# Two mixers that run on into their expert layers: normalising by token tile, turned tokens scaled in their copy, experts chosen on logits

## The reference

```
h = layer_norm(ALPHA * h + mix(h), ln_mix_g[l], ln_mix_b[l])     # mix: Mamba-2 (l = 0), differential attention (l = 1)
h = layer_norm(ALPHA * h + hier_moe(h), ln_ffn_g[l], ln_ffn_b[l])

def hier_moe(x):                                  # 4 groups of 8 experts, d_ff = 512
    g_prob = softmax(x @ w_group);  g_sel = argmax(g_prob)
    e_logits = (x @ w_expert)[the 8 of group g_sel]
    top_p, top_i = top_k(softmax(e_logits), 2);  top_p /= sum(top_p)
    weight = g_prob[g_sel] * top_p
    return sum over the 2 experts of weight * (silu(x @ w_gate[e]) * (x @ w_up[e])) @ w_down[e]
```

## The kernel before, in words

| step | engine | line |
|---|---|---|
| slots: mask of token to slot | VectorE | L958 |
| pick: gather the 32 tokens of e, turned, as h_rows x mask (32 passes) | TensorE | L966 |
| xg: copy them out of PSUM | ScalarE | L974 |
| gate and up product | TensorE | L981 |
| silu; times up; turn; copy (hT) | ScalarE, VectorE, TensorE, VectorE | L990, L996, L1002, L1010 |
| down product, and copy of its rows | TensorE; both | L1020, L1030, L1039 |

## Time and profile before

### The profile page before, as it was taken

One profiled execution on the slowest core, in us unless ns is written; L12 is line 12 of the kernel. 1 busy time (PEld: TensorE's weight loads), 2 busy tenths in 40 slices (PEclk: granted clock), 3 DMA queues, 4 the chain that ended last, 5 costly groups with the idle time before them and its releaser, 6 DMA issues. The chain is left out here.

```text
span 2371.8 us, 32407 instructions
## 1 busy us (share of the span) xinstructions
PE 2086.6 (88%) x13361; PEld 1391.1 (59%) x13361; DVE 690.8 (29%) x2051; ACT 372.8 (16%) x989; POOL 98.5 (4%) x96
## 2 busy tenths in 40 slices
PE   8999969999888697689888888697899989879997
PEld 7686456656556344366665565344588544448863
DVE  4355231111111316321111111367222014722211
ACT  2122111101111014011111111114121001312100
POOL 0112010000000100100000000100001000000110
PEclk9999957877888797778788888798899989889998
DMA  9332357999999941359999999631243333213420
GB/s 339 131 118 107 119 204 316 424 426 426 426 426 425 372 146 67 107 212 424 426 427 426 426 427 422 257 142 36 93 168 143 122 141 142 72 71 142 142 89 27
DMA packets 111421, 566.58 MB, mean 239 GB/s; under 512 B 11304, under 2 KB 14558, under 8 KB 78558
## 3 DMA queue, kind: packets, MB, share of 16 engines
q1 hardware_dynamic: 111326, 565.26, 59.8%
HBM read 564.19 MB, written 1.05 MB: 238 GB/s over the span
## 5 line engine op out<-in xcount | busy, mean ns | idle before, releaser
L981 PE MATMUL ps<-ring,arena 128*32 128x256 f32 x3968 | 261.9, 422 | 59.4 <-issue 38.4
L2148 PE MATMUL ps<-arena,ring 128*128 128x256 f32 x1408 | 308.0, 382 | 1.6 <-DVE arena L245 1.6
L2148 PEld LDWEIGHTS ps<-arena,ring 128*128 128x128 f32 x1408 | 270.0, 192 | 39.7 <-DVE arena L245 2.4
L966 PEld LDWEIGHTS ps<-arena 128*128 128x128 f32 x2048 | 247.6, 201 | 28.5 <-issue 25.5
L966 PE MATMUL ps<-arena 128*128 128x32 f32 x2048 | 255.1, 285 | 2.8 <-DVE arena L958 2.8
L1445 PE MATMUL ps<-ring,arena 128*128 128x512 f32 (+1 forms) x576 | 250.7, 595 | 2.5 <-DVE arena L245 1.6
L981 PEld LDWEIGHTS ps<-ring,arena 128*32 128x32 f32 x3968 | 154.9, 122 | 166.6 <-issue 115.3
L267 PE MATMUL ps<-ring,arena 128*128 128x512 f32 x544 | 236.8, 597 | 1.6 <-DVE arena L1485 0.8
L1020 PE MATMUL ps<-ring,arena 128*32 128x256 f32 x1984 | 179.3, 522 | 26.8 <-issue 25.8
L1445 PEld LDWEIGHTS ps<-ring,arena 128*128 128x128 f32 x576 | 110.1, 193 | 136.0 <-issue 132.3
L267 PEld LDWEIGHTS ps<-ring,arena 128*128 128x128 f32 x544 | 103.9, 192 | 131.7 <-issue 129.1
(11 more groups left out here) (297 smaller groups left out, 1713.8 us busy)
## 6 DMA issues: line engine op xcount, KB each, us to landing
ring<-in_moe_w_gate_dram SPq DMA_DIRECT2D x62, 2048.0 KB, 19.0
ring<-in_moe_w_up_dram SPq DMA_DIRECT2D x62, 2048.0 KB, 23.5
ring<-in_moe_w_down_dram SPq DMA_DIRECT2D x62, 2048.0 KB, 19.9
ring<-in_w_up_dram SPq DMA_DIRECT2D x22, 2048.0 KB, 7.8
ring<-in_ssm_w_in_dram SPq DMA_DIRECT2D x12, 2048.0 KB, 10.0
ring<-in_w_in_dram SPq DMA_DIRECT2D x10, 2048.0 KB, 13.5
ring<-in_w_down_dram SPq DMA_DIRECT2D x10, 2048.0 KB, 7.7
ring<-in_attn_w_qkv_dram SPq DMA_DIRECT2D x6, 2048.0 KB, 20.4
```

The lines of the kernel that those rows point to most:

```text
L966: mm = nc.tensor.matmul(ps[:, 4, k * CAP:(k + 1) * CAP], h_rows[:, tt, k, :], slots[:, b, tt, :], start=(tt == 0), stop=(tt == TT - 1))
L981: mm = nc.tensor.matmul(ps[j * CAP:(j + 1) * CAP, 5, 0:256], xg[:, b, k * CAP:(k + 1) * CAP], w[:, k, (j % 2) * 256:(j % 2 + 1) * 256], st ...
L2148: mm = nc.tensor.matmul(ps[:, n % 4, 0:SEQ], w[:, k, k4 * P:(k4 + 1) * P], xT_mlp[:, k, :], start=(k == 0), stop=(k == KD - 1))
```

## The change

- Expert layers have no block of their own. The functions of `moe` become `make_experts`, and each engine runs on from the mixer's stream into them; only the block ends after expert layers 0 and 1 are left.
- The norm is made per token tile. Tile 0 is summed, normalised and turned while TensorE still has products of tile 1 to do; for that the last pieces of the mixer's product are reordered. ScalarE normalises one half of the features of a tile, VectorE the other, without g and b, into `normed`, whose features are reordered in that write.
- `normed` is turned, and g and b are put in as scale and bias where the turned tokens are copied out of PSUM (`act_affine_T`, `dve_affine_T`; g and b are loaded as vectors along the partitions). GpSimd writes h = normed * g + b later (`pool_affine`), beside the first experts.
- The gathering reads `normed`, so the gathered tokens get g and b afterwards: VectorE makes xg by two instructions, where ScalarE made one copy.
- Groups and experts are chosen on the logits. The weights come from two exponential sums, exp(e_i - e_max) / (sum_group * sum_expert), made while TensorE gathers expert 0.
- ALPHA * h into PSUM moves from expert 0 to expert 3. Expert 1's weights and the router's are loaded earlier, where their places come free.
- From expert layer 0 to attention the same per-half norm and scaled copies are used; the qkv weights are loaded in the reordered row order.

Its core (`...` marks what is left out):

```diff
+        def pe_turn_normed(pe, tt, use=0):
+            pe.wait_ge(half_act.sem, half_act.at(2 * use + tt + 1))
+            pe.wait_ge(half_dve.sem, half_dve.at(2 * use + tt + 1))
+            for j in range(2):
+                for k in range(4):
+                    mm = nc.tensor.transpose(ps[:, 4 + 2 * tt + j, k * P:(k + 1) * P], normed[:, tt, 4 * j + k, :], ident)
+                mm.then_inc(n_turned.sem, 1)
+        def act_affine_T(act, tt, xT, which, use=0):
+            act.wait_ge(n_turned.sem, n_turned.at(4 * use + 2 * tt + 1))
+            for k in range(4):
+                ins = nc.scalar.activation(xT[:, k, tt * P:(tt + 1) * P], ps[:, 4 + 2 * tt, k * P:(k + 1) * P],
+                                           ACT.Identity, bias=vec[:, which, 1, k:k + 1], scale=vec[:, which, 0, k:k + 1])
+            ins.then_inc(xT_act.sem, 1)
+        def pool_affine(pool):
+            for tt in range(TT):
+                hv = h[:, tt, :].rearrange("p (q k) -> p k q", k=KD)
+                g, b = (rows_gb[:, i, :].rearrange("p (q k) -> p k q", k=KD) for i in range(2))
+                Q(nc.gpsimd.tensor_tensor(hv, normed[:, tt, :, :], g, ALU.mult))
+                ins = nc.gpsimd.tensor_tensor(hv, hv, b, ALU.add)
...
+            def dve_tokens(self, dve):
+                self.dve_sums(dve, 0, 0)
+                self.dve_sums(dve, 0, 1)
+                self.dve_norm(dve, 0)
+                self.dve_sums(dve, 1, 0)
+                dve.wait_ge(vectors_loaded.sem, 8 * 16)
+                dve_affine_T(dve, 0, xT_route, self.which)
+                self.dve_sums(dve, 1, 1)
+                self.dve_norm(dve, 1)
+                V(nc.vector.memset(lg, NEG))
+                self.dve_group(dve, 0)
+                dve_affine_T(dve, 1, xT_route, self.which)
+                self.dve_experts(dve, 0)
+                self.dve_group(dve, 1)
+                self.dve_experts(dve, 1)
+                dve.wait_ge(chosen.sem, chosen.at(2))
+                self.dve_positions(dve)
...
+            def step_xg(dve, s, v, prev, b):
+                dve.wait_ge(s["picked"].sem, v(s["picked"]))
+                if prev:
+                    dve.wait_ge(s["gateup"].sem, prev(s["gateup"]))
+                x = xg[:, b, :].rearrange("p (k c) -> p k c", k=KD)
+                nc.vector.tensor_tensor(x, ps[:, 4, 0:KD * CAP].rearrange("p (k c) -> p k c", k=KD),
+                                        bcast(g_mix, CAP), ALU.mult).then_inc(s["xg_scaled"].sem, 1)
+                dve.wait_ge(s["xg_scaled"].sem, v(s["xg_scaled"]))
+                nc.vector.tensor_tensor(x, x, bcast(b_mix, CAP), ALU.add).then_inc(s["xg"].sem, 1)
...
+                step_pick(pe, m, lambda s: s.at(1), 0)
+                head.pe_tally(pe)
+                for i in range(4):
+                    expert(0, i)
...
+                step_slots(dve, m, lambda s: s.at(1), None, 0, 0)
+                head.dve_weights(dve)
+                nc.vector.tensor_scalar(alpha_id, ident, ALPHA, None, ALU.mult).then_inc(alpha_ready.sem, 1)
+                step_xg(dve, m, lambda s: s.at(1), None, 0)
...
+            def experts_pool(pool):
+                pool.wait_ge(crowd.sem, crowd.at(1))
+                pool.wait_ge(half_act.sem, half_act.at(2))
+                pool.wait_ge(rows_loaded.sem, rows_loaded.at(32))
+                pool_affine(pool)
...
-                 ("out", 2, 0), ("out", 2, 1), ("out", 2, 2), ("turn_y", 6), ("turn_y", 7), ("out", 2, 3),
-                 ("out", 3, 0), ("out", 3, 1), ("out", 3, 2), ("out", 3, 3)]
+                 ("out", 2, 0), ("out", 2, 1), ("out", 2, 2), ("turn_y", 6), ("turn_y", 7),
+                 ("out", 3, 0), ("out", 3, 1), ("out", 2, 3), ("out", 3, 2), ("turn_normed", 0), ("out", 3, 3)]
...
+                for i, part in ((0, 0), (0, 1), (1, 0), (1, 1), (0, 2), (0, 3), (1, 2)):
+                    out_piece(i, part)
+                pe_turn_normed(pe, 0)
+                out_piece(1, 3)
+                head.pe_route(pe, 0)
+                pe_turn_normed(pe, 1)
+                head.pe_route(pe, 1)
+                head.pe_counts(pe)
+                experts.pe(pe)
```

More of the change, by code:

```diff
@@ L195, in hybrid_stack @@
         c_moe = [add_experts(0)]
-        c_qkv = [add(cols8(qkv_w, 512 * i, 512 * i + 512)) for i in range(6)]
+        c_qkv = [add(rows8_cols(qkv_w, 512 * i, 512 * i + 512)) for i in range(6)]
         c_wo = [add(rows4(o_w, i)) for i in range(2)]
@@ new lines, in dve_row_norm, with act_half @@
+        def dve_row_norm(tts):
+            mv, v, r = ln_mv[:, tts, :], ln_v[:, tts], ln_r[:, tts]
+            for tt in range(tts.start, tts.stop):
+                V(nc.vector.bn_aggr(ln_mv[:, tt, :], ln_stats[:, tt, :, :]))
+            V(nc.vector.tensor_scalar(v, mv[:, :, 1], EPS, None, ALU.add))
+            rsqrt(r, v, ln_t[:, tts])
+            return nc.vector.scalar_tensor_tensor(ln_b[:, tts], mv[:, :, 0], -1.0, r, ALU.mult, ALU.mult)
+        def act_half(tt, src, n_view):
+            return nc.scalar.activation(n_view, src, ACT.Identity, bias=ln_b[:, tt:tt + 1], scale=ln_r[:, tt:tt + 1])
@@ new lines, in dve_half @@
+        def dve_half(tt, src, n_view):
+            return nc.vector.tensor_scalar(n_view, src, ln_r[:, tt:tt + 1], ln_b[:, tt:tt + 1], ALU.mult, ALU.add)
+        def pe_turn_normed(pe, tt, use=0):
[5 more added lines that the diff above has]
+                mm.then_inc(n_turned.sem, 1)
@@ new lines, in act_affine_T, with dve_affine_T @@
+        def act_affine_T(act, tt, xT, which, use=0):
[4 more added lines that the diff above has]
+            ins.then_inc(xT_act.sem, 1)
+        def dve_affine_T(dve, tt, xT, which, use=0):
+            dve.wait_ge(n_turned.sem, n_turned.at(4 * use + 2 * tt + 2))
+            for k in range(4, 8):
+                ins = nc.vector.tensor_scalar(xT[:, k, tt * P:(tt + 1) * P], ps[:, 5 + 2 * tt, (k - 4) * P:(k - 3) * P],
+                                              vec[:, which, 0, k:k + 1], vec[:, which, 1, k:k + 1], ALU.mult, ALU.add)
+            ins.then_inc(xT_dve.sem, 1)
@@ new lines, in hybrid_stack @@
+        xT_first = area(6144, KD, SEQ)
+        STEP_SEMS = ("slots", "picked", "xg_scaled", "xg", "gateup", "silu", "hidden", "turned", "hT", "down", "rows_act",
+                     "rows_dve", "back", "back_turned", "back_copied")
+        MAIN = {n: sem("moe_" + n) for n in STEP_SEMS}
+        OVER = [{n: sem(f"over{layer}_" + n) for n in ("loaded", "shifted", "combined") + STEP_SEMS} for layer in range(2)]
+        alpha_ready, token_combined = sem("alpha_ready"), sem("token_combined")
+        w1_loaded, tail_stats = sem("w1_loaded"), sem("tail_stats")
@@ L715, in _ @@
                         copy_group(*s)
-                act_norm(act)
+                head.act_norm(act)
+                experts.act(act)
             @block.gpsimd
@@ L896, in _ @@
                 dve.wait_ge(dt_act.sem, 5)
-                dve_add_sums(dve, len(c_wout), True, 0)
-                dve_layer_norm(dve, lnp)
+                head.dve_tokens(dve)
+                experts.dve(dve)
         turn_done()
-        sums_done(len(c_wout))
-        norm_done()
-        W4 = 4 * CAP
-        route_pe, route_act, route_dve = sem("route_pe"), sem("route_act"), sem("route_dve")
-        router_loaded = sem("router_loaded")
-        STEP_SEMS = ("slots", "picked", "xg", "gateup", "silu", "hidden", "turned", "hT", "down", "rows_act",
-                     "rows_dve", "back", "back_turned", "back_copied")
@@ L1426, in hybrid_stack @@
-        moe(0, t["ln_ffn_g"][0], t["ln_ffn_b"][0])
+        summed.advance(3)
+        experts.done()
         projected, projected_copied = sem("projected"), sem("projected_copied")
```

1116 lines of the change are left out of this document (589 added, 527 removed).

## The result

Four runs of each kernel beside one another give 2337.4 us (2337.0 to 2338.4) for the changed kernel and 2366.5 us (2364.6 to 2372.5) for the kernel before: a ratio of 0.9873 with a 95% interval of 0.9854 to 0.9892, 29.1 us less. The second time that both ran side by side it was 2334.6 (2332.7 to 2336.0) and 2366.8 us, ratio 0.9865 (0.9844 to 0.9887). I had forecast 2327 us, range 2306 to 2344, from a gain of 38 us. The sign and the range hold; the gain was 9 us smaller. The profiled executions stand at 2373.6 and 2337.9 us (span 2371.8 and 2336.1).

What follows compares the result with a forecast made beforehand. The prediction took the weight stream to pace both expert loops, with TensorE just behind. Gains of 15, 16.5 and 6.5 us, 38 in all, off the 2364.99 us median gave 2327 us, range 2306 to 2344.

Steps and rivals of the forecast that it cites:

- What counts is when a stream starts: Expert loops: the weight stream paces them, so earlier starts gain about 15 us in layer 0, 16.5 us in layer 1.
- T to the first gate and up product, 26.9 us: Mixer-to-expert hand-over, from the last mixer product's end: 26.9 us against 43.5, a gain of 16.6 us.
- GpSimd's price: Behind expert 0's gathering: VectorE's x+b waits for GpSimd's whole operation, 2.2 us; an estimated 3.3 us by the skill's rule.
- T later by 2.3 and 1.2 us: End of the last mixer product: moved transposes delay it 1.2 us, and in the Mamba mixer ScalarE's copies another 1.1 us.
- The alpha products and DMA running dry: Layer 0: moving them off expert 4's load path saves 6.2 us, but DMA runs dry for 4.3 us, then 1 us.
- In the loop: cost nothing: Every expert: x*g and x+b, 1.0 us, hide beside the 1.93 us down product, leaving 0.9 us.
- Expert layer 0 to attention, 6.5 us: Third hand-over, to the first qkv product: 10.7 us against 17.2, a gain of 6.5 us.
- The sum: Whole kernel: gains of 15, 16.5 and 6.5 us make 38 us, giving 2327 us.
- 1 (clock stays full): Hand-overs: TensorE's clock stays at its full level, 8 and 6 us more gain, 2313 us; chance 0.17.
- 2: Hand-overs: GpSimd holds VectorE back more than once, costing 4 us a layer; gain 24 us, 2341 us; chance 0.15.
- 3: Expert loops: the streams have slack and starts don't count; only 6.5 us is left, 2358.5 us; chance 0.04.
- 4: Every expert: x*g and x+b outlast the down product, gate and up waits; slower, 2383 us; chance 0.04.

Runs made afterwards that it cites:

- experiment 3: Changed kernel with expert 4's gate and up loads issued only after expert 2's down product, both layers; 9.5 us above experiment 4.
- experiment 4: Changed kernel with expert 3's gate and up loads issued only after expert 0's down product, both layers; 2336.6 us.
- Experiment 8: Changed kernel with exponentials and routing weights put back ahead of positions and slot masks; 4.5 us above experiment 6.
- experiment 1: Changed kernel with GpSimd's scale and bias of h held until VectorE has made expert 1's slot masks; 2329.0 us.
- experiment 11: Changed kernel with eight extra unread x*g instructions on VectorE in every expert; 11.6 us slower than experiment 10.
- experiment 9: Changed kernel with the alpha*h products moved from expert 3 to expert 1, ahead of expert 4's load; 2334.4 us.
- experiment 10: Changed kernel with four extra unread x*g instructions on VectorE in every expert; 2333.5 us.
- Experiment 2: Changed kernel with unread filler products (8, 3, 5, 1, 4) in TensorE's gaps at both mixer-to-expert hand-overs; time moved by 1.3 us.
- experiment 5: The kernel before, run again unchanged; 2366.8 us.
- experiment 6: The changed kernel, run again unchanged; 2334.6 us.
- experiment 12: Changed kernel with unread TensorE fillers (5, 2, 3, 1, 2) and GpSimd's second tile held behind expert 3's masks; 2325.5 us, 0.9831 of the kernel before.

## Why the prediction was right, and where its numbers were off

**What counts is when a stream starts: right, with the wrong mark named.** Experiments 3 and 4 show it. I had computed with expert 4's load as well as with the first gate and up product; only the first is the start.

**T to the first gate and up product, 26.9 us: the terms right, two sized too small.** Measured 28.67, four times within 0.02. By terms: to the router's start 9.2 (8.2), router 3.6 (3.5), selection 2.7 (2.4), count, positions and masks 1.4 (1.3), gathering 7.0 (7.0), behind it 4.7 (3.9); 0.6 us for semaphores is inside these. The two mis-sized terms: ScalarE's permuted half took 1.31 us instead of 1.0 and TensorE waited 3.89 us for it, and scale and bias took 1.37 to 1.51 instead of 1.2; behind the gathering, GpSimd's operation was 2.87 instead of 2.2 us. The gain is 14.9 us where I had 16.6. Experiment 8 shows 3.1 us of it, the weights. For the rest, the block's end and the norm by token tile, no run takes one of them out alone: their share is read from the timelines.

**GpSimd's price.** The operations took 2.87 us (scale, L422) and 3.86 to 3.99 us (bias, L423, two operands with a step of 32 bytes), against 2.2 us in order. The Trainium skill (GPSIMD Engine Reference, Performance pitfalls for Q7 kernels) puts some 50% on reads of SBUF with a step over 8 bytes, an estimated 3.3 us: this trace has 30% with one such input and about 77% with two, so the page was nearer than my figure.

That VectorE waits for the whole operation is shown by experiment 1. Held back were x+b, with both inputs in SBUF, and the masks' tensor_scalar, all in SBUF; x*g, with one input in PSUM, took 0.43 us beside GpSimd's 3.86 us at 331.28 in experiment 1. The Trainium skill (SBUF — State Buffer, Who interferes with whom) says that tensor_scalar can contend with GpSimd for a shared pair of ports, and that an operation with two inputs in SBUF contends with GpSimd's reads, while one with at most one input in SBUF, outside the two-port modes, does not. The trace agrees: 2.73, 4.04 and 0.43 us.

**T later by 2.3 and 1.2 us: the first too small.** The end of the Mamba mixer's product, before:

```profile
275.30 0.63 PE L592 MATMUL ps<-cst,arena 128*128 128x128 f32 x4 [1.02 <-ACT arena L693]
275.76 17.33 PE L607 MATMUL ps<-ring,arena 128*128 128x512 f32 x40
```

and in the changed kernel:

```profile
270.97 0.63 PE L1250 MATMUL ps<-cst,arena 128*128 128x128 f32 x4 [1.02 <-ACT arena L1358]
272.62 15.67 PE L1265 MATMUL ps<-ring,arena 128*128 128x512 f32 x32 [1.02 <-ACT arena L1358]
```

From the first of these rows to T it is 17.8 us in both profiles of the kernel before and 21.6 us in the changed kernel: 3.8 us later. The turn and the second pause of 1.02 us are there as I had them. With them alone it is 19.9 us, 2.1 later, which is what experiments 3 and 11 have, at a clock of 1.00. In the ten other profiles of changed code the clock falls to its lower level once, within 1 us of the end of the second pause (mean 0.92 from 270 to 292 us, where the kernel before has 1.00), and that is the other 1.7 us. In the attention mixer, from the start of w_out's products to T, it was 29.9 us at a clock of 0.92 and is 28.6 us at 1.00 in five profiles of changed code, the two of the changed kernel among them, and 30.7 to 30.9 in seven. So with a like clock T is 0.9 us later there, and in the changed kernel it came 1.3 us earlier.

**The alpha products and DMA running dry: a wrong step.** I took their 6.2 and 3.7 us off the path and gave most of it back (5.3 us in layer 0) to a stream that runs dry ahead of expert 5's down load. Neither happened. From L4 to expert 31's load it is 388.3 and 387.6 us before, 387.9 twice after: it does not run dry. And G to L4 is 30.9 and 31.0 us after, where three of the four cases of before have 31.0 to 32.0 with the products inside. Without them TensorE spends more of that stretch at half clock; experiment 9 puts their worth at 2 us a layer. That the two errors nearly cancel (I kept 0.7 and 1.1 us) is luck.

**In the loop: cost nothing, right.** In experiment 10 x+b comes 1.4 us later (four times 0.34) and costs nothing that can be measured, so the room is more than the 0.9 us that I had counted.

**Expert layer 0 to attention, 6.5 us.** Measured 17.15 to 11.20 us, 6.0 us. The terms were 10.7 in sum, 0.5 us too little. They leave out SyncE: in eight of the twelve profiles of changed code this hand-over takes 11.8 to 13.2 us, and there the next block begins 0.65 us after SyncE's last issue for the qkv weights ends. Experiment 2:

```profile
784.58 3.76 SPq L114 DMA_DIRECT2D ring<-in_attn_w_qkv_dram  x1
...
785.39 1.36 DVE L419 TENSOR_SCALAR arena<-ps,tiny 128x128 f32<-128x128 f32 x4 [0.34 <-PE ps L401]
...
789.05 1.19 PE L1598 MATMUL ps<-ring,arena 128*128 128x512 f32 x1 [3.70 <-PEq L1113]
```

The scaled copies end at 786.75, the issue at 788.34, and the block only then. The last three issues take SyncE 3.8 to 6.2 us each, where one in the loop takes 0.3 to 0.4. So the block end that the change left here cost up to 2 us more than I had counted.

**The sum.** In the second pair (experiments 5 and 6) the gain is 13.4 us (layer 0) and 14.9 us (layer 1) at L4, and 6.4 us at attention (17.55 to 11.19), 34.7 us; less 3.8 us by which T came later in the Mamba mixer, and 1.3 us more in the attention mixer: 32.2 us. The medians of that pair differ by 32.0 us, those of the first by 29.1; the other stretches between the marks differ by 1 to 3 us either way, in code that is the same. My 38 us had 3.4 us too much in the two terms to the first gate and up product, 1.8 us kept of the alpha products, and 0.5 us at attention. The 35.7 us between the two first profiles contain the 6 us by which layer 0 of the kernel before was dear. That the clock cost 1.7 us in one mixer and gave about as much back in the other is luck again.

**Rivals.** 1 (clock stays full) did not happen by itself; experiment 12, which brings most of it about and holds GpSimd back besides, takes 13.5 us off the two T>L4 and 8 us off the time; I had given the clock alone 14. 2 happened in part: x+b and both masks waited, but the masks ended inside the product and the gathering was not late. 3 is refuted by experiment 3. 4 is refuted by experiments 10 and 11, which also show that its price per 0.1 us was set too high.

## What to carry to other kernels

Find the one transfer with which the stream stops pausing, and price every edit by what it does to that issue; a load that merely comes first may have slack (here at least 7 us). Behind an idle stretch price TensorE work at half clock, and expect that removing work there gives back less than its length. Before giving GpSimd a large SBUF operation, list the SBUF-only instructions of VectorE that fall beside it, and start it behind them.

## What the runs showed of the hardware

In experts 0 to 3 the granted clock alternates although TensorE hardly pauses: 29.87 of 31 us busy at a mean of 0.78, with the gathering passes of expert 1 at full clock (3.76 us) and expert 0's down product behind them at half (3.55 us; at full clock it takes 1.93). With the clock held at 1.00 through the hand-over it was 0.83 afterwards, so it is not only the idle time ahead that lowers it. Where exactly it switches differed between executions; with that, T>L4 of the kernel before differed by up to 8 us, more than most parts of this change are worth.
